# Sending out the mixed activations of a feed-forward stage two groups at a time

## The reference

```python
def swiglu(h, w_gu, w_down):
    gu = h @ w_gu
    gate, up = jnp.split(gu, 2, axis=-1)
    return (jax.nn.silu(gate) * up) @ w_down

h = rms_norm(x, norm_ffn_pre_g[l])
f = (jax.nn.silu(h @ w_gate[l]) * (h @ w_up[l])) @ w_down[l]
```

## Time and profile before

| what | value |
|---|---|
| median of three runs | 1968.66 us (1966.41 to 1970.02) |
| profiled execution | 1967.67 us, its span 1965.9 us |
| mean granted clock of TensorE | 0.988 |
| busy share of the span: PE, PEld, DVE, ACT, POOL | 97%, 82%, 63%, 43%, 25% |

### The profile page before, as it was taken

How to read it: one execution, slowest core, us unless ns; L and a number is a source line. 1 busy time by engine, 2 the same in 40 slices (tenths; PEclk the granted TensorE clock), 3 DMA queues, 4 the chain that set the end, 5 groups by cost and what they waited for, 6 DMA issues and landing times. The chain is left out here.

```text
span 1965.9 us, 27808 instructions
## 1 busy us (share of the span) xinstructions
PE 1908.2 (97%) x10930; PEld 1612.4 (82%) x10930; DVE 1238.5 (63%) x1866; ACT 851.8 (43%) x1453; POOL 493.5 (25%) x419
## 2 busy tenths in 40 slices
PE   9999999997999999979999999999999997999998
PEld 7777788876899898768998988777887786899897
DVE  6677545378467465774674666887654457467465
ACT  5344433454244244442442456665543344244244
POOL 4110002115143231342332342222010025143230
PEclk9999999998999999989999999999999998999999
DMA  6122233331433233223343332222232231433223
GB/s 174 55 65 65 70 100 107 111 90 56 118 90 109 86 105 110 86 69 103 87 118 90 99 103 74 65 66 65 86 97 65 76 93 56 118 87 109 86 79 104
DMA packets 340788, 176.57 MB, mean 90 GB/s; under 512 B 6481, under 2 KB 339378, under 8 KB 340658
## 3 DMA queue, kind: packets, MB, share of 16 engines
q1 hardware_dynamic: 340658, 174.79, 30.7%
HBM read 172.67 MB, written 2.10 MB: 89 GB/s over the span
## 5 line engine op out<-in xcount | busy, mean ns | idle before, releaser
L1868 DVE TENSOR_TENSOR WL<-RAW,WH 128x1024 fp32r<-128x1024 f32 (+3 forms) x371 | 415.6, 1126 | 251.9 <-ACT WH L1577 248.7
L1577 ACT ACTIVATE WH<-RAW 128x1024 fp32r<-128x1024 f32 (+3 forms) x371 | 326.4, 886 | 384.3 <-PE ps L1336 329.9
L1332 PE MATMUL ps<-HH,WH 128*128 128x512 f32 x1152 | 461.5, 401 | 0.9 <-ACT HH L1624 0.9
L1336 PE MATMUL ps<-HL,WH 128*128 128x512 f32 x1152 | 449.7, 390 | 0.8 <-DVE HL L1950 0.8
L1334 PE MATMUL ps<-HH,WL 128*128 128x512 f32 x1152 | 449.2, 390 | 0.7 <-DVE WL L1868 0.7
L1332 PE MATMUL ps<-GH,WH 128*128 128x512 f32 x688 | 269.3, 391 | 0.0
L1336 PE MATMUL ps<-GL,WH 128*128 128x512 f32 x688 | 267.9, 389 | 0.0
L1334 PE MATMUL ps<-GH,WL 128*128 128x512 f32 x688 | 267.8, 389 | 0.0
L1332 PEld LDWEIGHTS ps<-HH,WH 128*128 128x128 f32 x1152 | 216.4, 188 | 53.3 <-issue 8.2
L1336 PEld LDWEIGHTS ps<-HL,WH 128*128 128x128 f32 x1152 | 216.3, 188 | 49.2 <-DVE HL L1950 2.1
L1334 PEld LDWEIGHTS ps<-HH,WL 128*128 128x128 f32 x1152 | 216.5, 188 | 48.0 <-issue 4.1
(11 more groups left out here) (251 smaller groups left out, 3062.3 us busy)
## 6 DMA issues: line engine op xcount, KB each, us to landing
RAW<-in_ffn_w_gu SPq DMA_DIRECT2D x88, 512.0 KB, 3.8
RAW<-in_w_in SPq DMA_DIRECT2D x67, 512.0 KB, 3.7
RAW<-in_ffn_w_down SPq DMA_DIRECT2D x32, 512.0 KB, 3.7
RAW<-in_w_gate SPq DMA_DIRECT2D x22, 512.0 KB, 3.9
RAW<-in_w_up SPq DMA_DIRECT2D x22, 512.0 KB, 3.8
RAW<-in_w_out SPq DMA_DIRECT2D x16, 512.0 KB, 3.9
RAW<-in_mem_w_kv SPq DMA_DIRECT2D x16, 512.0 KB, 3.8
RAW<-in_w_down SPq DMA_DIRECT2D x16, 512.0 KB, 3.7
```

The costliest lines, as they stand in the source:

```text
L1332: e.matmul(bk, wh, xh, start=k == 0, stop=False)
L1336: last = e.matmul(bk, wh, xl, start=False, stop=k == kt - 1)
L1577: e.activation(at.weight(n, "H"), at.raw(n), ACT.Copy).then_inc(*sg.inc("hi", n))
L1868: e.tensor_tensor(at.weight(n, "L"), at.raw(n), at.weight(n, "H").bitcast(F32), ALU.subtract).then_inc(*sg.inc("lo", n))
```

## The change

The table is changed in one line, for all three stages: groups 0 and 1 are mixed behind the first plain tile, groups 2 and 3 behind the second, and none behind the others. The instructions are the same ones.

```diff
-MIX_AT = ((0,), (1,), (2,), (3,), ())
+MIX_AT = ((0, 1), (2, 3), (), (), ())
 PLAIN = len(MIX_AT)
```

## The result

The changed kernel takes 1973.65 us (median of ten runs, 1970.88 to 1974.18) against 1968.71 for the kernel before (ten runs, 1966.41 to 1970.02): a ratio of 1.0027, with a 95% interval of 1.0019 to 1.0036, so 4.9 us slower. The profiled execution has a span of 1971.1 us, 5.2 more than before.

A forecast was written before the change was run, and what follows sets the result against it. A chain through DVE, ACT and POOL to PE's product 5 was taken to bound each stage: 7.86 - 1.16 - 4.28 - 0.3 = +2.12 us a stage, +6.4 in three, giving 1975.0 us (range 1968.0 to 1981.0).

The forecast's parts named there:

- product 5: Point in the first pair (1662.21, third stage) whose passing by PE was priced; behind it nothing stops PE for long.
- the wait of 8.26: PE's idle time before the last mix is split, in the third stage's first pair (1641.34 to 1649.88); not priced.
- Leg 1: DVE's first normal to the end of the last plain projection's weight split: 26.99 to 34.85, +7.86 us (+6.2 to +9.5).
- The turns at memory: DVE and POOL excluding each other at SBUF; taken as +0.27 us a tile, bounds 0 and 1.1.
- Leg 2: From that weight split to tile 3's product (L2077), which waits for POOL's gate_r: 8.96 to 7.80, -1.16 us.
- leg 3: Tile 3's product to the first place split, with two normals, a mix and its splits gone: 9.35 to 5.07, -4.28.
- leg 4: First place split to PE passing product 5, one POOL operation fewer beside the splits: 10.90 before, -0.3 us (0 to -0.6).
- a shift there passes to the end one to one: Claim that any delay at product 5 reaches the kernel's end in full, in each of three stages.
- The cover: PE's stand after products 0 and 1 until place, over 4 us, hiding anything late on PE itself.
- The last rival: Slower by the clock: granted clock falls to 0.52 behind PE's new stops, +4.0 us a stage, 1987.0; chance 0.07.
- The second mix hides: Faster: second mixes don't lengthen the first stretch, 1951.4, or one hides, 1962.2; decides below 5.7 us growth; chance 0.08.
- No change: Turns at memory fall well and the last weight split meets no combination, -2.7 at most a stage; 1969.0; chance 0.19.

The follow-up runs named there:

- e1: Changed kernel with POOL's subtractions of mixes 1 and 3 covering 32 of 256 columns; 1962.64 us against 1967.28 for the kernel before, ratio 0.9976.
- e3: Half of the change: one double tile only (mixes 1 and 2 together, mix 3 a tile earlier); 1965.87 us against 1967.28 for the kernel before, 0.9995.
- e4: Changed kernel with the planner looking 7 instead of 8 ahead for combinations, putting two behind tile 3's gate_r; 1966.95 us against 1967.28 before, 0.9998.
- e6: Kernel before the change with the planner's look-ahead for combinations 7 instead of 8, no other edit; 1962.35 us against 1967.74, ratio 0.9971.
- e2: Changed kernel with the splits of the mixes behind the up projection's weight split instead of ahead; 1973.10 us against 1967.28 for the kernel before, 1.0032.
- e5: All four mixes placed behind tile 0, their splits in tile 1; 1972.17 us against 1967.74 for the kernel before, ratio 1.0022.

## Why the prediction was right

**The time.** The forecast was 1975.0 us, +6.4; measured are 1973.65 and +4.9.

**What bounds the kernel.** Pricing product 5 and not the wait of 8.26 was right. That wait went away in all three stages and the kernel became slower.

**Leg 1** was forecast at 34.85 and is 34.87. Its pieces hold too. The next normals come 15.30 after the first (forecast 15.23). The two mixes end 10.45 after the first normal (10.39). The weight split follows 1.72 behind them, as read before, and the last one takes 2.29 beside a combination (2.31). The turns at memory cost what I took, near the lower bound: four normals take 3.22, where two pairs alone would take 2.82, and the two mixes take 8.91 on POOL (1611.05 to 1619.96) against 2 x 4.29. The Trainium skill's "SBUF — State Buffer", section "Who interferes with whom", would make one of two such instructions wait in full; the 1.72 of L2327 beside the 1.75 of L1868 agrees (0.73 and 1.21 where neither meets the other). But by that rule for every normal the sum would have gone to its upper bound, and all turns of a double tile's pass come to 0.34 (15.30 against 10.67 + 4.29): what DVE loses at its normals and its first weight split isn't added, because its last NL split waits for the second mix by way of ACT in any case (1.29 in front of 1620.65). e1 shows POOL's part of this leg, 3.56 of the 7.88.

**Leg 2** was forecast at 7.80 and is 7.95, **leg 3** at 5.07 and is 5.10, **leg 4** at 10.60 and is 10.48 (the eight place splits take 6.65 in place of 7.07). e3 shows leg 3's gain by itself, and e4 that leg 2 is a wait for POOL.

**Sum.** +2.12 a stage was forecast; +2.16, +1.83 and +2.20 came. The smaller one lies with the kernel before, whose second stage was longer; in the changed kernel the three differ by 0.07.

**The step that was mis-sized** is "a shift there passes to the end one to one". Of +6.19 at the three products, +5.20 arrives at the end: 0.64 is lost between the first and the second stage (from 331.87 to 331.23 between product 5 and the next first normal), 0.15 added before the third (734.39 to 734.54), and 0.50 lost after it. In the kernel before, PE has a stop in a later pair of the first stage:

```profile
623.22 0.39 PE L1360 MATMUL ps<-HH,WH 128*128 128x256 f32 x1 [0.64 <-DVE TS L1907]
```

and one of 0.61 at 1802.45 in the third. In the changed kernel PE has no stop of over 0.25 us in either place: it comes there later, and waits that much less for DVE.

**The cover was mis-sized too**, without effect on the time. PE's stops in the plain tiles (0.76, 1.07, then 1.74 and 1.82) are about the 1, 1.4 and 4 forecast. But the first product comes 43.44 after the first normal, not 40.3: from 1639.89 to 1645.42 thirteen matmuls take 5.53 us, 0.43 each against 0.22 before (33.00 / 148), which is 2.6 us. In the first two stages the same pair of stops was followed by eight such matmuls. So the stop in front of product 2 is 2.73, 2.80 and 1.56 in the three stages, not over 4. A granted clock well under 1.00 in the plain tiles stands among the prediction's own signs of being wrong, and it came: 0.55 from 1640 to 1646, the 1.2 GHz level but for the end of the stretch. As a sign it failed, for the time didn't follow it. The last rival had priced a whole slow projection, at 5.4 us or 1.0 more than the cover; about half a projection came, and the cover took all of it.

**The rivals.** *The second mix hides* fails by leg 1, +7.88 against the 5.7 from which it would decide. *No change* needed 2 us of luck in the turns, and the last split free of a combination; neither came.

## What to carry to other kernels

Price a reorder at the point where the engine that bounds the kernel last waits, by the chain of the other engines up to there, and not by the longest wait in the list: an 8 us wait can be cover. Moving work ahead in in-order queues cost about its full time here (4.6 us for a mix of 4.29) to everything queued behind it, and paid once, where it no longer stood; so the first double tile was free (e3) and the second cost 2.3 us a stage. When a queue holds work that nothing needs yet ahead of work that a chain needs (here sums of weights on POOL, ahead of gate_r in e4 and ahead of a mix in e6), that order is worth a try before the larger move.

## What the runs showed of the hardware

The granted clock fell behind shorter stops than the 8.26 us of the kernel before: in the changed kernel behind two stops of 1.74 and 1.82 us close together (0.55 in the window of 6 us that follows in the third stage, 0.72 and 0.75 in the first two), in e2 behind one of 2.19 (0.81), in e5 behind one of 4.64 (0.50). Behind a single stop of 1.74 us in e3 it stayed at 1.00:

```profile
1632.00:1640.00 8.00, 6.65 (x28) 5.17 (x29) 6.98 (x7) 1.87 (x3) 6.65 (x5) 1.00 0.23 68
```

The Trainium skill's page "TensorE: Matmul & The Clock Gate", section "HAM oscillation — how this bites in real kernels", tells of idle stretches between bursts that bring the lower clock back; the stop of 4.64 agrees, and of stops as short as the others that section has no example. At what length of stop it begins these runs don't settle: the same pair of stops brought different lengths of low clock in the three stages.
